# An expert block on one core: the loads of the second expert weight issued by GpSimd in place of SyncE

## The reference

```
for e in range(N_EXPERTS):                       # 32
    z = einsum('bsd,df->bsf', h, w1[e]) + b1[e]  # w1[e]: 1024 x 2048
    glu = minimum(z[..., 0::2], 7.0); lin = clip(z[..., 1::2], -7.0, 7.0)
    act = glu * sigmoid(1.702 * glu) * (lin + 1.0)
    out = out + combine[..., e:e+1] * (einsum('bsf,fd->bsd', act, w2[e]) + b2[e])   # w2[e]: 1024 x 1024
```

## Time and profile before

| | |
|---|---|
| time, median of 3 | 1135.33 us (1135.15 to 1137.33) |
| span of the profiled execution | 1132.6 us |
| PE / DVE / ACT / POOL busy | 1061.5 / 266.0 / 181.5 / 17.4 us |
| DMA | 430.91 MB, mean 380 GB/s over the span |
| q1, hardware queue of SyncE | 84068 packets, 427.36 MB, 93.2% of 16 engines' span |
| q0, software queue of GpSimd | 416 packets, 1.57 MB, 0.4% |
| w1 loads, w2 loads | 256 and 128 of 1024 KB, median 20.6 and 23.1 us from issue to landing |
| chain that ended last | PE 55%, DMA 22%, SyncE's queue 20% |

### The profile page before, as it was taken

One profiled execution on the slowest core, in us unless ns is written; L12 is line 12 of the kernel. 1 busy time (PEld: TensorE's weight loads), 2 busy tenths in 40 slices (PEclk: granted clock), 3 DMA queues, 4 the chain that ended last, 5 costly groups with the idle time before them and its releaser, 6 DMA issues.

```text
span 1132.6 us, 12620 instructions
## 1 busy us (share of the span) xinstructions
PE 1061.5 (94%) x4658; PEld 400.5 (35%) x4658; DVE 266.0 (23%) x694; ACT 181.5 (16%) x323; POOL 17.4 (2%) x20
## 2 busy tenths in 40 slices
PE   8899998999999999998989999998989898989895
PEld 7548644333333333332323222232323232323221
DVE  3446344122221212121212111111212121212122
ACT  3411233111111111111011111111111111101112
POOL 0320000000000000000000000000000000000000
PEclk8999998999999999999999999999999999999999
DMA  9773593999999999999999999999999999999995
GB/s 303 218 264 149 237 394 118 393 415 417 400 418 418 418 417 417 418 417 418 418 417 416 418 418 418 418 418 419 417 418 417 418 418 417 417 418 417 418 416 217
DMA packets 85722, 430.91 MB, mean 380 GB/s; under 512 B 8912, under 2 KB 10500, under 8 KB 52836
## 3 DMA queue, kind: packets, MB, share of 16 engines
q1 hardware_dynamic: 84068, 427.36, 93.2%
q10 hardware_dynamic: 1216, 1.70, 0.8%
q0 software_dynamic: 416, 1.57, 0.4%
HBM read 427.98 MB, written 2.62 MB: 380 GB/s over the span
## 4 chain that ended last, share of the span: by engine, by line
PE 55%; DMA 22%; SPq 20%; issue 1%; DVE 1%; ACT 0%; DVEq 0%; ACTq 0%
PE ps L1095 22%; DMA w1r<-w_mlp 19%; SPq L239 12%; PE ps L1124 8%; SPq L236 7%; PE ps L909 5%; PE ps L1140 4%; PE ps L921 4%; PE ps L1071 3%; DMA w2r<-w_mlp 3%; PE ps L1003 1%; PE ps L1032 1%; PE ps L1078 1%; PE ps L1103 1%; PE ps L1148 1%
## 5 line engine op out<-in xcount | busy, mean ns | idle before, releaser
L1095 PE MATMUL ps<-w1r,arena 128*64 128x512 f32 x2048 | 484.1, 600 | 22.7 <-DMA w1r<-w_mlp 21.5
L1124 PE MATMUL ps<-w2r,arena 128*64 128x512 f32 x1024 | 233.4, 597 | 24.6 <-DMA w2r<-w_mlp 24.6
L1095 PEld LDWEIGHTS ps<-w1r,arena 128*64 128x64 f32 x2048 | 131.6, 136 | 294.7 <-issue 215.1
L1124 PEld LDWEIGHTS ps<-w2r,arena 128*64 128x64 f32 x1024 | 69.3, 136 | 178.1 <-issue 110.0
L830 DVE TENSOR_TENSOR acc<-ps,acc 128x512 f32<-128x512 f32 x64 | 41.2, 686 | 204.6 <-PE ps L1140 204.6
L822 DVE TENSOR_TENSOR arena<-arena 128x512 f32<-128x512 f32 x32 | 22.1, 692 | 224.5 <-ACT arena L511 224.5
L520 ACT ACTIVATE arena<-ps 64x512 f32<-64x512 f32 x32 | 18.9, 591 | 333.0 <-PE ps L1124 333.0
L1140 PE MATMUL ps<-arena 128*128 128x512 f32 x128 | 63.2, 617 | 1.3 <-ACT arena L522 1.3
L1071 PE MATMUL ps<-h,arena 128*64 128x512 f32 x256 | 62.2, 607 | 1.1 <-DVE arena L790 1.1
L788 DVE TENSOR_SCALAR sel_z<-small 96x64 bf16 (+1 forms) x32 | 6.1, 191 | 242.3 <-PE ps L1095 242.2
L909 PE MATMUL ps<-w1r,h 128*128 128x512 f32 x128 | 56.8, 603 | 0.0
(11 more groups left out here) (205 smaller groups left out, 551.5 us busy)
## 6 DMA issues: line engine op xcount, KB each, us to landing
w1r<-w_mlp SPq DMA_DIRECT2D x256, 1024.0 KB, 20.6
w2r<-w_mlp SPq DMA_DIRECT2D x128, 1024.0 KB, 23.1
w1r<-w_in SPq DMA_DIRECT2D x7, 2048.0 KB, 20.7
w1r<-w_out SPq DMA_DIRECT2D x2, 2048.0 KB, 10.4
rel_table<-arena ACTq DMA_DIRECT2D x1, 1536.0 KB
acc<-x SPq DMA_DIRECT2D x2, 512.0 KB, 4.5
arena<-rel_table POOLq DMA_DIRECT2D x1, 1024.0 KB, 12.2
out<-w1r SPq DMA_DIRECT2D x2, 512.0 KB, 2.6
```

Source lines behind the costliest of these rows:

```text
L1095: ins = mm(ps[64 * c:64 * c + 64, 2 * par + n, :], hgT[:, par, k % 4, 64 * (k // 4):64 * (k // 4) + 64], w1r[:, 8 * par + k, at:at + 512], ...
L1124: ins = mm(ps[at:at + 64, 4 + c, :], actT[:, k % 4, 64 * (k // 4):64 * (k // 4) + 64], w2r[:, k // 2, col:col + 512], start=False, stop=(k ...
```

## The change

`load_w2` and `next_w2` go from SyncE's program to the end of GpSimd's. The waits that guard each load are the same ones. SyncE keeps the w1 loads, in the same order among themselves and with the same waits. On GpSimd the w2 loads of all 31 later experts are one loop. The weights' slots, the work of TensorE, VectorE and ScalarE, and all sizes stay as they are.

```diff
@@ SyncE
-            def load_w2(e, c):
-                sp.dma_start(w2r[:, c, :].rearrange("p (a d) -> p a d", a=2), w2_v[e, c]).then_inc(w2_in[c], 16)
...
-            sp.wait_ge(L_ready, 4)
-            sp.wait_ge(qkbT_tr, 4)
-            for c in range(4):
-                load_w2(0, c)
...
             def rest_of_sweep(base):
                 next_w1(base, 2, 0)
                 next_w1(base, 3, 1)
-                next_w2(base, 1)
-                next_w1(base, 4, 0, range(0, 4))
-                next_w2(base, 2)
...
-                with sp.Fori(3, NE // 2) as m:
+                with sp.Fori(2, NE // 2) as m:
                     next_w1(base, 2 * m, 0)
-                    next_w2(base, 2 * m - 1)
                     next_w1(base, 2 * m + 1, 1)
-                    next_w2(base, 2 * m)
-                next_w2(base, NE - 1)
@@ GpSimd, behind the adds that make L
+            def load_w2(e, c):
+                pool.dma_start(w2r[:, c, :].rearrange("p (a d) -> p a d", a=2), w2_v[e, c]).then_inc(w2_in[c], 16)
+
+            def next_w2(base, e):
+                for c in range(4):
+                    pool.wait_ge(w2_used, 4 * base + (4 * (e - 1) + c + 1))
+                    load_w2(e, c)
+
+            pool.wait_ge(L_ready, 4)
+            pool.wait_ge(qkbT_tr, 4)
+            for c in range(4):
+                load_w2(0, c)
+            with pool.Fori(1, NE) as e:
+                next_w2(0, e)
+            pool.wait_ge(sweeps_ready, 1)
+            n = pool.value_load(n_sweeps[0:1, 0:1], min_val=1, max_val=SWEEPS)
...
```

More of the change, by code:

```diff
@@ L298, in next_w1 @@
                     load_w1(e, k, 8 * par + k)
[L300 to L303, removed]
             def rest_of_sweep(base):
@@ L331, in _ @@
                     next_w1(base, 0, 0)
-                    next_w2(base, 0)
                     next_w1(base, 1, 1)
@@ L377, in _ @@
                 ins.then_inc(L_ready, 1)
+            def load_w2(e, c):
[12 more added lines that the diff above has]
+            n = pool.value_load(n_sweeps[0:1, 0:1], min_val=1, max_val=SWEEPS)
+            with pool.If(n > 1):
+                with pool.Fori(1, n) as r:
+                    base = pool.snap(r * NE)
+                    with pool.Fori(0, NE) as e:
+                        next_w2(base, e)
         @block.scalar
```

## The result

| | before | after |
|---|---|---|
| time, median | 1135.8 us (4 runs, 1135.15 to 1137.33) | 1162.22 us (4 runs, 1157.71 to 1164.98) |
| ratio | | 1.0217, 95% interval 1.0193 to 1.024 |
| span of the profiled execution | 1132.6 us | 1160.2 us (device time 1161.85) |

The change costs 26.4 us; forecast were 21.5, a time of 1157. I read the page of the kernel after first: granted clock and GB/s in 40 slices, the packets, the two queues with packets, MB and share, and the two weight groups with busy, mean ns and idle time.

A forecast was written before the change was run, and what follows sets the result against it. Weight loads at 418 GB/s were taken as the limit. To 1135.3 us came 20.4 us at the end and about 1 for GpSimd's later first packet: 1157 us, own range 1148 to 1166, 8 in 10 from 1136 to 1176.

The forecast's parts named there:

- The bound: Expert loop: weight loads at 418 GB/s are the limit, 30.1 us per expert against TensorE's 26.9.
- the one dent: Rate dip to 339 GB/s at 285 to 290 us; nearly all that freeing SyncE can win, called 1 us.
- First expert early: Before the expert loop: w2(0) leaves at about 78 us instead of 124.60; worth 0 us.
- The division of the engines: Loop: two busy queues alternate packet by packet, so w2 gets a third of the bytes, 139 GB/s.
- The even flow: Loop: TensorE waits for w2 from the second expert, down projections 30.1 us apart, w2 landings about 30 us.
- R1: Rival: w2 gets half or more of the engines, w1 gates, the end's order turns; 1141 us, chance 0.20.
- Where the loss is: End of the sweep: w1 runs out first, engines idle between w2 loads waiting for slots; +20.4 us.
- The rest of the end: down(29) to down(31): TensorE at its own pace, last matmul ending at 1139.6 instead of 1119.2 us.
- The 1 us set aside for it: Last expert: GpSimd's preparation of rows, its later first packet, between 0 and +6 us, taken as 1.
- R2: Rival: no change, w2 falls only some loads behind w1 and the end stays; 1134 us, chance 0.09.
- R3: Rival: two queues hide gaps between 4 KB packets, the loop runs at 424 GB/s; 1128 us, chance 0.10.
- R4: Rival: dearer software-queue packets, 176 ns, +28 us over the loop; 1185 us at the upper bound, chance 0.07.

The follow-up runs named there:

- act_queue: Kernel before, with w2 loads of experts 1 to 31 moved to ScalarE's hardware queue, w2(0) staying on SyncE; 1160.84 us, ratio 1.0212.
- w2wide_sp: Kernel before, all loads on SyncE, with w2 read in runs of 8 KB for each partition instead of two of 4 KB; 1126.70 us, ratio 0.991.
- half_sp: Kernel before, all loads on SyncE, with experts 16 to 31 left out; 653.93 us.
- w2wide_pool: Changed kernel (w2 on GpSimd) with w2 read in runs of 8 KB for each partition; 1133.06 us, ratio 0.997 to the kernel before.
- w1split_pool: Changed kernel (w2 on GpSimd) with each w1 load cut into two DMAs, so packets of 4 KB; 1162.88 us, ratio 1.0232 to the kernel before.
- act_split: act_queue with each w2 load cut into two DMAs of 512 columns, 2 KB packets; 1193.48 us, ratio 1.0505 to the kernel before.
- half_pool: Changed kernel (w2 on GpSimd) with experts 16 to 31 left out; 677.87 us.
- w2split_sp: Kernel before, all loads on SyncE, with each w2 load cut into two DMAs of 512 columns, 2 KB packets; 1152.65 us, ratio 1.0158.

## Why the prediction was right, point by point

**The bound.** Right. 418 GB/s before and after, and the one dent was worth about what was said; nothing was to be won by freeing SyncE. SyncE waited 177 us for slots of w2; now it waits 743 us for slots of w1, and the rate in the middle is the same. The waits of SyncE's queue and of TensorE after (us in total, times, longest):

```profile
SPq L236 <- PE ps L1091: 742.7, 240, 19.2
```

```profile
PE ps L1120 <- DMA w2r<-w_mlp: 64.6, 22, 5.5
```

**First expert early.** Right, 0 us (act_queue). TensorE starts down(0) at 230.6 in place of 228.8 us, but that is scatter: it is 229.0 in act_queue, 229.8 in w2wide_sp and 232.9 in half_sp, where the prologue is nearly the same.

**The division of the engines.** Right while both queues have work, and it is the step on which all rests. Packets go one to one between two queues (376 to 379, and 176 to 176 with 2 KB beside 8 KB), the share follows from the packets' sizes (w2wide_pool, w1split_pool, act_split), and this holds for a hardware queue as for the software one (act_queue). What the prediction read from 462 packets in four microseconds of the prologue carried the whole sum.

**The even flow.** Wrong, with little effect on the sum. I had w2 at a steady third, with landings of some 30 us and down projections 30.1 us apart. The median landing is 18.0 us, and the starts alternate: down(2)'s use of its first quarter comes 37.4 us after down(1)'s (257.58 and 295.00), down(1)'s 24.4 after down(0)'s (233.17). An expert takes 30.2 us only in the mean. w1 keeps running out of free slots (743 us of waits), and then w2 gets far more than a third, as from 300 to 310 us. So the sign I gave for R1, w2 landing in 20 us or less, was a bad one: it came true, while TensorE waited for w2 alone, as forecast.

**Where the loss is.** Right: at the end (half_pool), as w1's lead, two experts of loads that came too early. The direct trial, w2 on GpSimd with w1 held back so that it has no lead, was not run. The rate halves between 1090 and 1100 us; 1089 was said. w2(28) was to gate down(28) at 1077. Here the size was off: the last wait is already that for w2(27), at 1051.33 us, and from there TensorE is alone. The timeline and a window of it:

```profile
1051.33 3.60 PE L1120 MATMUL ps<-w2r,arena 128*64 128x512 f32 x8 [5.27 <-DMA w2r<-w_mlp]
...
1077.21 7.04 PE L1120 MATMUL ps<-w2r,arena 128*64 128x512 f32 x32
```

```profile
1051.33:1054.75 3.42, 3.42 (x8) 0.95 (x10) 0.00 (x0) 0.00 (x0) 0.00 (x0) 0.50 1.03 423
```

An odd step lasts 29.3 us by itself, so almost no wait is left in it; nearly all the waiting of two experts falls on the even one (22 waits in 64.6 us, where I had one for each expert in mind).

down(28) ends at 1084.25 (1077.21 + 7.04) and not at 1078.7, the largest miss of the sum. By the forecast's own terms w2(27) is in at 230.75 + 3.5 + 27 x 30.1 = 1046.95; it came at 1051.33, 4.4 us later. Of these, 2.5 were there at w2(1), in at 266.87 in place of 264.35, since its first load was issued at 233.17 and not at 230.75; the other 1.9 are 26 experts at 30.17 us and not 30.1. Then 1.7 us are the quarter at clock 0.50, that is 1.2 GHz, after a pause of 5.3 us (3.42 us in place of 1.72). Less the 0.7 by which a gate at w2(27) would have let down(28) end earlier than the one at w2(28) that I had, this is 5.4 of the 5.6 us. That waits this long bring the clock down was a term I had left out. In the middle it does not show in the rate, which is 418 GB/s at a mean clock of 0.96 as at 1.00.

**The rest of the end.** down(29) ends 24.4 us later (24.4 said), down(30) 27.6 (27.4 said), and the last matmul 10.5 (9.1 said). The last w2 load was issued 0.6 us after down(30)'s end, at 1136.96, and took 7.8 us to land and not 6.1; that is 2.4 us, of which the sum had 1.3 to spare, so 1.1 of the 1.4. The 1 us set aside for it is nearly that. 1139.6 was said for the last matmul, 1146.8 it is: 7.2 us more, 6.2 after that microsecond; the medians are 5.2 apart. So the mechanism was right and the sum too low by about a fifth.

**The rivals.** R1 was the right price for the wrong packets. R2 took the rule of the Trainium skill (DMA: Bandwidth & Descriptors, section on issuing engines) for it, that another issuer only saves issue time. The measurements agree with its first half, no bandwidth is gained or lost (418 and 418); but that nothing else changes, as R2 had it, is wrong here, because the order of arrival does, by 26 us. Of the Trainium skill's other rule (the same page, section on queues, rings and completion order) the traces agree with the turns by packet, one to one; how many descriptors a packet holds they don't show, and turns of whole loads, which the prediction made of it, did not happen. R3 and R4 would have shown in the middle's rate, and it didn't move. R4's 176 ns for a packet of the software queue belonged to packets of 512 B pieces; from 444 to 1080 us after,

```profile
q0 software_dynamic: 22860, 88.12, 34.6%
```

a packet took 154 ns on average (34.6% of 16 x 636 us over 22860, some small packets among them).

## What to carry to other kernels

Where transfers are the limit, the order in which weights arrive counts beside their rate, and one queue in the order of use keeps it. Two queues divide the engines by packets while both have work, so here the stream with the shorter rows fell behind, and the other's lead was worthless at the end. That w2 also has fewer slots than w1 is part of the explanation, but no run changed the number of slots. The row length is the better lever: 8 KB instead of 4 KB runs for w2 gave 9 us, and 16 KB runs for w1 on top of it 14 in all, for a changed view of the same weights.

## What the runs showed of the hardware that I had not expected

A GpSimd DMA put two rows of 2 KB into one packet of 4 KB (146 packets for 0.53 MB), where SyncE's and ScalarE's kept a packet for each (176 packets for 0.34 MB in act_split; 120539 packets in w2split_sp in place of 85722). The loop's rate by length of run, on one queue: all 4 KB 410 GB/s, 8 KB with 4 KB 418, all 8 KB 422, 16 KB with 8 KB 426. A pause of 5.3 us of TensorE was followed by 3.4 us at half clock, and the changed kernel, with such pauses in its loop, has a mean granted clock of 0.96 there.
